# Two gaps in the SBUF layout of a float32r encoder trunk: the activation tiles 384 bytes further on, modulo 512 bytes

## What is computed

```python
D_MODEL, SEQ, DEPTH, D_FF = 1024, 256, 2, 2816

def swiglu(x, w_gate, w_up, w_down):
    a = jnp.einsum('bsd,df->bsf', x, w_gate)
    u = jnp.einsum('bsd,df->bsf', x, w_up)
    return jnp.einsum('bsf,fd->bsd', jax.nn.silu(a) * u, w_down)

def reference(x, ...):
    for l in range(DEPTH):
        x = x + 0.5 * swiglu(rmsnorm(x, ffn1_norm[l]), ffn1_w_gate[l], ffn1_w_up[l], ffn1_w_down[l])
        x = x + hybrid_mixer(rmsnorm(x, mix_norm[l]), w_in[l], ..., w_out[l])
        x = x + 0.5 * swiglu(rmsnorm(x, ffn2_norm[l]), ffn2_w_gate[l], ffn2_w_up[l], ffn2_w_down[l])
    return rmsnorm(x, final_norm)
```

## Time and profile before

| | us |
|---|---|
| median of three runs | 964.71 |
| lowest and highest | 963.52, 965.16 |
| the profiled execution, its own time | 965.2 |
| its span, first to last instruction | 963.2 |
| TensorE (PE) busy | 950.4 |
| PE's weight loads (PEld) busy | 942.7 |
| VectorE (DVE) busy | 613.3 |
| ScalarE (ACT) busy | 456.5 |

### The profile page before, as it was taken

The page is one execution under the profiler, slowest core; times in us unless marked ns, Lnnn a source line. Parts: engine busy times, 40 slices in busy tenths (PEclk is TensorE's granted clock), DMA queues, the critical chain, the costliest instruction groups (busy, mean ns, idle before and its releaser), DMA issues.

```text
span 963.2 us, 19406 instructions
## 1 busy us (share of the span) xinstructions
PE 950.4 (99%) x8188; PEld 942.7 (98%) x8188; DVE 613.3 (64%) x732; ACT 456.5 (47%) x490; POOL 2.8 (0%) x6
## 2 busy tenths in 40 slices
PE   8999999999999999999999999999999999999996
PEld 8999999999999999999999999999999999999996
DVE  6756555587758665555686555557786785555653
ACT  6433443457645433443554344346584634334332
POOL 0000000000000000000000000000000000000001
PEclk9999999999999999999999999999999999999997
DMA  8665565553246665555556555555522665656621
GB/s 284 216 216 176 184 203 180 178 179 118 77 153 200 210 202 175 185 195 187 174 191 209 174 186 194 186 177 167 183 66 70 216 220 189 203 174 190 201 87 44
DMA packets 130613, 169.05 MB, mean 176 GB/s; under 512 B 3216, under 2 KB 116112, under 8 KB 130576
## 3 DMA queue, kind: packets, MB, share of 16 engines
q1 hardware_dynamic: 130576, 168.52, 54.4%
HBM read 167.46 MB, written 1.05 MB: 175 GB/s over the span
## 4 chain that ended last, share of the span: by engine, by line
PE 93%; DVE 3%; ACT 2%; DMA 1%; issue 0%; SPq 0%; POOL 0%; DVEq 0%
PE ps L356 29%; PE ps L357 29%; PE ps L358 29%; PE ps L413 1%; PE ps L563 1%; DMA raw<-in_ffn_w_gate 1%; PE ps L576 1%; DVE resid L1048 0%; DVE wlo L1021 0%; PE ps L722 0%; ACT sq L812 0%; ACT whi L791 0%; PE ps L700 0%; DVE work L1291 0%; DVE xlo L1026 0%
## 5 line engine op out<-in xcount | busy, mean ns | idle before, releaser
L1021 DVE TENSOR_TENSOR wlo<-raw,whi 128x2048 fp32r<-128x2048 f32 (+1 forms) x159 | 355.9, 2239 | 252.9 <-ACT whi L791 252.9
L356 PE MATMUL ps<-xhi,whi 128*128 128x256 f32 x1680 | 471.9, 281 | 0.0
L357 PE MATMUL ps<-xlo,whi 128*128 128x256 f32 x1680 | 470.7, 280 | 0.0
L358 PE MATMUL ps<-xhi,wlo 128*128 128x256 f32 x1680 | 469.3, 279 | 0.0
L791 ACT ACTIVATE whi<-raw 128x2048 fp32r<-128x2048 f32 (+1 forms) x159 | 297.3, 1870 | 166.1 <-PE ps L358 160.1
L356 PEld LDWEIGHTS ps<-xhi,whi 128*128 128x128 f32 x1680 | 316.2, 188 | 1.7 <-issue 1.0
L357 PEld LDWEIGHTS ps<-xlo,whi 128*128 128x128 f32 x1680 | 315.9, 188 | 0.0
L358 PEld LDWEIGHTS ps<-xhi,wlo 128*128 128x128 f32 x1680 | 315.0, 187 | 0.0
L356 PE MATMUL ps<-h_parts,whi 128*128 128x256 f32 x768 | 212.7, 277 | 0.0
L357 PE MATMUL ps<-h_parts,whi 128*128 128x256 f32 x768 | 212.4, 277 | 0.0
L358 PE MATMUL ps<-h_parts,wlo 128*128 128x256 f32 x768 | 212.3, 276 | 0.0
(11 more groups left out here) (150 smaller groups left out, 485.5 us busy)
## 6 DMA issues: line engine op xcount, KB each, us to landing
raw<-in_ffn_w_down SPq DMA_DIRECT2D x44, 1024.0 KB, 4.9
raw<-in_ffn_w_up SPq DMA_DIRECT2D x43, 1024.0 KB, 5.3
raw<-in_ffn_w_gate SPq DMA_DIRECT2D x42, 1024.0 KB, 5.4
raw<-in_w_in SPq DMA_DIRECT2D x12, 1024.0 KB, 5.2
raw<-in_w_in SPq DMA_DIRECT2D x8, 512.0 KB, 4.6
raw<-in_w_out SPq DMA_DIRECT2D x8, 512.0 KB, 4.4
raw<-in_w_in SPq DMA_DIRECT2D x2, 1088.0 KB, 5.2
raw<-in_ffn_w_gate SPq DMA_DIRECT2D x8, 256.0 KB, 7.1
```

The lines of the kernel that those rows point to most:

```text
L356: pe.matmul(o, w_hi, x_hi, start=start, stop=False, skip_group_check=True)
L357: pe.matmul(o, w_hi, x_lo, start=False, stop=False, skip_group_check=True)
L358: return pe.matmul(o, w_lo, x_hi, start=False, stop=stop, skip_group_check=True)
L1021: nc.vector.tensor_tensor(lo, r, h.bitcast(F32), ALU.subtract).then_inc(lo_done, 1)
```

## The change

Two tensors that nothing reads or writes are declared, of 96 and 32 floats in each partition.

```diff
         rs_v = sb("rs_v", [P, 8])
         rs_t = sb("rs_t", [P, 8], I32)
+        sb("gap_x", [P, 96])
         xhi = sb("xhi", [P, KT, SEQ], F32R)
         xlo = sb("xlo", [P, KT, SEQ], F32R)
         sq = sb("sq", [P, KT, SEQ])
...
         mx = sb("mx", [P, HEADS, 2])
+        sb("gap_h", [P, 32])
         h_parts = sb("h_parts", [P, 4, FT, SEQ], F32R)
```

## The result

The changed kernel takes **959.24 us**, the median of 14 runs (952.3 to 964.02). The kernel before took 965.75 us in its 14 runs of the same comparison (963.1 to 969.54). The ratio is **0.9928, 95% interval 0.991 to 0.9945**: faster by 0.7%. I had forecast 943.3 us, in a range of 940 to 955. The forecast is wrong: 16 us off, with a third of the expected gain. The spread is a result too: 11.7 us between the fastest and the slowest run of one program, against 6.4 us before.

What follows compares the result with a forecast made beforehand. TensorE's stream of matmuls was taken to bound the kernel. Terms of -22.2, -0.2, +0.4 and +0.6 sum to -21.4 us, giving 943.8 from the profiled 965.2 and a median forecast of 943.3 us, range 940 to 955.

Steps and rivals of the forecast that it cites:

- The sharpest test: Mixer's token unit M_V0, now at distance 64: pace should rise from 113.4 to about 117.8 ns, 0.4 us more.
- the changed kernel's 5040 matmuls with `xhi` and `xlo` run as M_V0 does now: Gate, up and projection units: each matmul falls from 117.8 to 113.4 ns, 22.2 us less.
- memory: First 96 `h_parts` matmuls in `w_out`, both layers: slow pace inherited from the unit before might go; 0.2 us less taken.
- `h_parts`. Its distance is unchanged, and 40 of its 44 full FFN units need nothing.: FFN down units: distance stays 192, so 40 of 44 full units keep their pace, no change in time.
- caught half way: Rival: 448 allows the fast pace, but whole units stay slow depending on how they are entered; about 954 us, chance 0.08.
- the 0 that I had put: Mixer's M_V1: distances only change places among k-tiles, so 0, with 0.6 us either way.
- the term of 0.6 us: Mixers: PE's gain turns into longer waits before `rcol` (0.2 us) and `sq` (0.1 us), 0.6 us given back over two layers.
- the other tensors that moved by 384: `sq`, `par`, `cst`, `work`, `rB`, touched by DVE, ACT and small matmuls: taken as 0, at most 0.5 us either way.
- The half-clock stretch: 3.4 us at half clock after the second mixer's attention may go, stay or recur: 1.4 us either way.
- 448 is worse: Rival: gate, up and projection matmuls slow to 120.0 ns, 11.1 us more, 975.8 us; chance 0.06.
- 448 is better than 192: Rival: 5040 matmuls run below 113 ns, 935.5 us at 112 ns, down to 909; chance 0.02 for better than 940.
- no change: Rival: distance doesn't decide; the two paces come from something else, such as buffer or PSUM tile; 964.7 us, chance 0.08.

Runs made afterwards that it cites:

- experiment 1: Separate kernel outside the reference: blocks of 48 matmuls at distances 0 to 480 bytes, four entries each, plus blocks with both operands shifted; 586.18 us.
- experiments 1 to 8: Follow-up runs: separate matmul kernels mapping pace by distance, and variants of the kernel before with only xhi/xlo or h_parts moved, or xhi/xlo at 0 or 288; trunk variants 957.49 to 976.3 us.
- e_x0: Kernel before with xhi and xlo moved to distance 0 modulo 512 and h_parts kept at 192; 976.3 us, ratio 1.0082.
- experiment 2: The separate distance-map kernel again, with ScalarE copies and VectorE subtractions running beside its matmuls; 586.18 us.
- e_gapx: Kernel before with only the first gap of 96 floats: xhi and xlo at 448, h_parts at 64; 957.49 us, ratio 0.991.
- e_plus3: Kernel before with three extra unread matmuls (xhi moving) ahead of each down unit in the FFN loops; 978.79 us, one run.
- experiment 10: Changed kernel plus eight unread matmuls at distance 0 ahead of the first down unit of each FFN; 949.68 us, ratio 0.9845.
- experiment 9: Kernel before with xhi, xlo and h_parts all placed 112 bytes from the weights modulo 256; 944.85 us, ratio 0.9786.
- the bench: Separate kernel outside the reference, timing rows of matmuls of one shape at chosen operand distances; its first map took 586.18 us.

## Why the prediction was wrong, step by step

**Right: PE's pace bounds the kernel, and the distance matters.** Gate and up of FFN 3 run at the forecast's pace (10.88 us for 96, where 10.9 was asked for). The sharpest test came out as put: M_V0 rose to the slow pace. Its matmuls 4 to 48, in the timeline of the changed kernel:

```profile
239.28 0.28 PE L358 MATMUL ps<-whi,xhi 128*128 128x256 f32 x1
...
244.47 0.28 PE L360 MATMUL ps<-whi,xlo 128*128 128x256 f32 x1
```

5.19 us / 44 = 118.0 ns (from 113.4 in the earlier trace rows), in both layers: 0.4 us more, the term of the sum. Since 64 and 448 both can have both paces, this test is weaker than I had called it; the shifted blocks of experiment 1 are the better one.

**Wrong: "the changed kernel's 5040 matmuls with `xhi` and `xlo` run as M_V0 does now".** This step took a distance to have one pace. It was the term of 22.2 us; 8.6 us of it came in the traced run. 64 and 448 were read as "slow" and "fast" from one sample each, and both have both phases (experiment 1). The evidence lay in the earlier trace rows, where `h_parts` runs at 117.7 and 113.4 ns at one address. I saw it, called it memory, and sized it at 0.2 us, because I applied it only to the 96 matmuls in which it was already visible.

**Wrong: "`h_parts`. Its distance is unchanged, and 40 of its 44 full FFN units need nothing."** They did: 1584 more of its matmuls became slow, 6.8 us. Their pace had never been theirs alone. In the kernel before, X at 64 and H at 192 are in different classes, so a phase was taken anew at each change of unit, and with the same 96 matmuls in between H took the same one each time, in the traced run the fast one. That was not certain either: three of the kernel's runs beside experiments 1 to 8 took 973.0 to 974.4 us at a mean clock of 0.993, where its others at that clock took 965.1 to 968.2; none of the three was traced. 448 is the class of 192: now nothing changes from unit to unit, and what the entry into an FFN draws holds until its end. The two ways in look alike. Timeline of PE in the changed kernel at the entries into FFN 2, which became slow, and FFN 3, which became fast:

```profile
309.57 0.60 PE L415 MATMUL ps<-cst,rs_y 128*128 128x128 f32 x4
309.93 0.37 PE L358 MATMUL ps<-xhi,whi 128*128 128x256 f32 x1
310.13 0.28 PE L359 MATMUL ps<-xlo,whi 128*128 128x256 f32 x1
310.25 0.28 PE L360 MATMUL ps<-xhi,wlo 128*128 128x256 f32 x1
```

```profile
497.03 0.61 PE L415 MATMUL ps<-cst,rs_y 128*128 128x128 f32 x4
497.39 0.37 PE L358 MATMUL ps<-xhi,whi 128*128 128x256 f32 x1
497.60 0.28 PE L359 MATMUL ps<-xlo,whi 128*128 128x256 f32 x1
497.71 0.28 PE L360 MATMUL ps<-xhi,wlo 128*128 128x256 f32 x1
```

The same four small matmuls, the same first start 0.36 us behind them; then steps of 0.12 us in one and of 0.11 to 0.12 in the other. In the trace's nanoseconds they part at once: the first two steps are 204 and 119 ns in FFN 2, 206 and 116 in FFN 3.

**The rival "caught half way" was the one that came**, in its mechanism, at 0.08 and 954 us. Its price lacked what H can lose. Against the kernel before, the 11 groups of an FFN that enters fast save 11 x 96 x 4.4 ns = 4.6 us, and those of one that enters slow cost 11 x 48 x 4.3 ns = 2.3 us. FFN by FFN 6.9 us are at stake on one draw.

The 14 runs bear this out. Each also has its own mean granted clock, 0.991 to 0.995, and in e_x0 0.004 of that mean went with 3.8 us, so that 0.001 is worth some 1 us. As an estimate, brought to a clock of 0.996 by that, the runs fall into three groups: four at 949 to 950 us, six at 955 to 957, four at 961 to 962, with the traced one in the last. Steps of 5 to 6 us are near the 6.9 of one FFN, so three, two and one fast FFN are the likely reading, and the median stands for two; only one run was traced.

**The waits.** PE's two waits in the first mixer, changed kernel:

```profile
210.35 0.29 PE L360 MATMUL ps<-whi,xlo 128*128 128x272 f32 x1
210.91 0.46 PE L415 MATMUL ps<-cst,rcol 128*128 128x128 f32 x2 [0.27 <-DVE rcol L1076]
...
266.35 0.28 PE L360 MATMUL ps<-xhi,wlo 128*128 128x256 f32 x1
266.99 0.35 PE L724 MATMUL ps<-ones,sq 128*128 128x1 f32 x2 [0.36 <-ACT sq L950]
```

From start to start 0.56 us instead of 0.60 before `rcol`, and 0.64 instead of 0.54 before `sq`. The second is the 0.1 that I had put; for the first, 0.2 longer, M_KV would have had to be fast. M_V1 took 6.36 us from its first start to its last (6.38 before), the 0 that I had put. With changes this small the term of 0.6 us was never really tried. **The rest held**: other engines kept their means (DVE's split 2238 ns), no new wait of PE for DVE showed up in the mixer, and the other tensors that moved by 384 cost nothing visible. The half-clock stretch is not in the profiled execution: 1.4 us, within its bound.

**The other rivals.** "448 is worse" has no trace; no block or unit at 448 settled at 120. "448 is better than 192" has none either: nothing ran below 113.3 ns. The 109.2 ns put beside it come from a formula that the Trainium skill (TensorE: Matmul & The Clock Gate, "Back-to-back issue gap") gives for an isolated matmul; for a stream of weight loads and matmuls, as here, the same section says that both set the pace. The Trainium skill's rule that I weighed for "no change" (SBUF — State Buffer, "Who interferes with whom": PE has two read ports and never waits) agrees with experiment 2, where DVE and ACT changed no block's pace by more than 0.04 ns. It doesn't cover what decided here: the runs show a pace that hangs on the distance between PE's own two operands, 113.3 to 123.3 ns for one shape at full clock.

**What stays open.** Why two phases exist, and why 64 and 192 can be as fast as 113.3 ns and their neighbours not, no run explains. What picks the phase at a break isn't known either: FFN 1 of e_gapx entered slow where the other three entered fast (and the narrow spread of its runs argues that it always does), FFN 1 of e_plus3 began slow where that of the kernel before began fast, and FFNs 2 and 3 of the changed kernel part behind entries whose first step differs by 2 ns. Whether those 2 ns are the cause or already the effect is not shown. I can set a phase by force (experiment 10) or avoid the choice (experiment 9), but not predict it.

## What to carry to other kernels

When one shape of matmul shows two paces in one trace, collect all stretches of it, with their distance and with what came before each, and ask of every "fast" reading whether the place or the history made it so; an unmoved neighbour whose pace depends on history is part of the change. Read PE's pace from start distances or from counts in equal stretches, never from its busy share. And prefer a layout whose pace showed no dependence on the entry: here 112 bytes between moving and stationary operand gave 944.85 us in a spread of 3 us, where the better-looking 448 gave 959.24 in a spread of 12.

## What the runs showed of the hardware

- The pace of 128 x 128 x 256 float32r matmuls with a load each depends on the distance between the operands' starts modulo 256 bytes: 120.0 ns at 0, 116.6 to 117.8 at 32, 118.7 at 128, 113.3 at 112, and 113.3 or 117.8 at 64 and 192. Traffic of ACT and DVE, tried for distances 0 to 416, changed none of it.
- The two phases at 64 and 192 hold over hundreds of matmuls, through changes of buffer within a class. In long rows of the bench a switch from the slow phase at 64 to 192 landed in the fast one behind a multiple of three matmuls and else not (12 of 12 rows of 36 to 47 matmuls, and 11 of 11 of 14 to 24 behind a wait). In the trunk a multiple of three repeated the pace of the group before, fast or slow.
- Thirty-two matmuls more, in the right places, took the changed kernel from 959.24 us (ratio 0.9928 to the kernel before) to 949.68 us (0.9845), though they are 3.8 us of work of their own.
